# A MoE router with the tokens in the partitions, and a first expert that is selected straight from the counts

## What is computed

```python
def moe_ffn(h, w_router, w_gate, w_up, w_down):
    logits = (h @ w_router).astype(jnp.float32)
    top_logit, top_idx = lax.top_k(logits, TOP_E)
    gates = jax.nn.softmax(top_logit, axis=-1)
    combine = jnp.sum(jax.nn.one_hot(top_idx, N_EXP, dtype=jnp.float32) * gates[..., None], axis=-2)
    out = jnp.zeros_like(h)
    for e in range(N_EXP):
        out = out + combine[..., e:e + 1].astype(h.dtype) * swiglu(h, w_gate[e], w_up[e], w_down[e])
    return out
...
            h = h + moe_ffn(rms_norm(h, od_norm_ffn[i]), od_w_router[i], od_w_gate_e[i], od_w_up_e[i],
                            od_w_down_e[i])
```

## Time and profile before

| | us |
|---|---|
| three runs | 1521.80, 1523.29, 1526.05; median 1523.29 |
| the profiled execution | 1521.72, its span 1519.9 |
| PE busy in the span | 1431.6 (94%) |
| DVE, ACT, POOL busy | 1176.7, 1000.3, 74.6 |
| first transpose of x of block 1 | at 486.66 |
| first matmul of `gather_first` | at 505.09 |
| first matmul of `job(0)` | at 518.93 |

### The profile page before, as it was taken

The page is one execution under the profiler, slowest core; times in us unless marked ns, Lnnn a source line. Parts: engine busy times, 40 slices in busy tenths (PEclk is TensorE's granted clock), DMA queues, the critical chain, the costliest instruction groups (busy, mean ns, idle before and its releaser), DMA issues.

```text
span 1519.9 us, 18914 instructions
## 1 busy us (share of the span) xinstructions
PE 1431.6 (94%) x6676; PEld 1172.7 (77%) x6676; DVE 1176.7 (77%) x1139; ACT 1000.3 (66%) x975; POOL 74.6 (5%) x101
## 2 busy tenths in 40 slices
PE   7988999999888699999999999999999999999996
PEld 6766888887666578878878878887887887887885
DVE  5854555556554698889888888889888988888887
ACT  6554643435564577777777777787777777777776
POOL 1010100001341200000000000000000000000000
PEclk9999999999999699999999999999999999999998
DMA  9511865545332499999989989999999999998993
...
DMA packets 218360, 438.49 MB, mean 288 GB/s; under 512 B 7230, under 2 KB 11376, under 8 KB 218320
## 3 DMA queue, kind: packets, MB, share of 16 engines
...
...
## 4 chain that ended last, share of the span: by engine, by line
PE 86%; DVE 6%; issue 4%; ACT 3%; POOL 1%; DMA 0%; DVEq 0%; ACTq 0%; POOLq 0%
PE bank L1572 26%; PE bank L1567 26%; PE bank L1568 26%; DVE w_lo L952 2%; PE bank L2144 2%; ACT w_hi L436 1%; POOL pr L903 1%; PE bank L1742 1%; PE bank L2182 1%; PE bank L1801 1%; DVE w_lo L945 0%; PE bank L2098 0%; PE bank L2106 0%; PE bank L1808 0%; DVE key_mask L1127 0%
## 5 line engine op out<-in xcount | busy, mean ns | idle before, releaser
L952 DVE TENSOR_TENSOR w_lo<-raw,w_hi 128x2048 fp32r<-128x2048 f32 x339 | 768.7, 2288 | 84.4 <-ACT w_hi L443 83.2
L443 ACT ACTIVATE w_hi<-raw 128x2048 fp32r<-128x2048 f32 x339 | 649.5, 1919 | 185.5 <-PE bank L1572 185.5
L1567 PE MATMUL bank<-w_hi,xg_hi 128*128 128x512 f32 x896 | 355.4, 397 | 0.6 <-issue 0.6
L1568 PE MATMUL bank<-w_hi,xg_lo 128*128 128x512 f32 x896 | 350.2, 391 | 0.0
L1572 PE MATMUL bank<-w_lo,xg_hi 128*128 128x512 f32 x896 | 241.3, 391 | 10.1 <-DVE w_lo L952 10.1
L1567 PE MATMUL bank<-w_hi,ht_hi 128*128 128x512 f32 x528 | 207.4, 393 | 2.5 <-issue 2.5
L1568 PE MATMUL bank<-w_hi,ht_lo 128*128 128x512 f32 x528 | 206.5, 391 | 0.0
L1572 PEld LDWEIGHTS bank<-w_lo,xg_hi 128*128 128x128 f32 x896 | 168.0, 188 | 48.6 <-DVE w_lo L952 13.5
L1567 PEld LDWEIGHTS bank<-w_hi,xg_hi 128*128 128x128 f32 x896 | 168.8, 188 | 35.2 <-issue 0.7
L1568 PEld LDWEIGHTS bank<-w_hi,xg_lo 128*128 128x128 f32 x896 | 169.0, 189 | 33.7
L945 DVE TENSOR_TENSOR w_lo<-raw,w_hi 128x2048 fp32r<-128x2048 f32 (+4 forms) x65 | 144.4, 2232 | 43.9 <-ACT w_hi L436 43.8
...
## 6 DMA issues: line engine op xcount, KB each, us to landing
...
```

The lines of the kernel that those rows point to most:

```text
L443: act.activation(w_hi[:, g % HL, :], raw[:, g % RAW, :], ACT.Copy).then_inc(hi_ready, 1)
L952: dve.tensor_tensor(w_lo[:, g % HL, :], raw[:, g % RAW, :], w_hi[:, g % HL, :].bitcast(F32), ALU.subtract)\
L1567: pe.matmul(out_ap, l_hi, r_hi, start=first, stop=False)
L1568: pe.matmul(out_ap, l_lo, r_hi, start=False, stop=False)
```

## The change

The tokens become the stationary operand of the router, 128 of them at a time, and the 8 columns of `w_router` the moving one; so the logits come out with the tokens in the partitions, block by block, and no copy and no transpose are needed. `router(0)` stands before the transposes of block 1. DVE does `two_best(b)` for each block. The counting matmuls take float32r operands (`tri_r`, `ones_r`, `chose_r`), whose zeros and ones are exact, and one pass each. `sel` of the first expert is made from its own column of the counts; the rest of `spot`, then `place`, the gates and the over-full experts follow behind it on DVE. `xn` is now x times the gain row (from DVE, before the root is known), and the inverse root comes in as a scale where `xn_hi` and `xn_lo` are made; the gather is done for all of `xn_hi` first and for `xn_lo` after it into banks of its own, so that `xg_hi` and `xg_lo` are plain copies. ACT scales `xn` for the scatter, which POOL did before. The first three expert tiles are split earlier or elsewhere: `job_lo(0, 0)` before block 0 is filled, `job_lo(0, 1)` between the two `two_best`, `job_lo(0, 2)` behind the copies of `xg_lo`. The gain row is loaded without a wait for `x_added`.

```diff
+            act.activation(ident_r, ident, ACT.Copy).then_inc(wr_split, 1)
...
+            job_hi(0, 0)
             fill_block(0, lambda c: G_FFN1 + c)
+            job_hi(0, 1)
             fill_block(1, lambda c: G_FFN1 + c)
             act.wait_ge(x_added, 8)
             token_squares(6)
             root(6, 2)
+            act.wait_ge(inv_ready, 8)
             for b in range(T):
-                act.wait_ge(src_ready, b + 1)
-                act.activation(xn_hi[:, b], xn[:, b], ACT.Copy).then_inc(xn_split, 1)
-            act.activation(ident_r, ident, ACT.Copy).then_inc(wr_split, 1)
-            for i in range(AHEAD):
-                job_hi(0, i)
-            act.wait_ge(chosen, 1)
+                act.wait_ge(rows_gained, b + 1)
+                act.activation(xn_hi[:, b], xn[:, b], ACT.Copy, scale=stat[:, 6 + b:7 + b]).then_inc(xn_split, 1)
+            job_hi(0, 2)
+
+            for k in range(2):
+                act.wait_ge(hi_gathered, k + 1)
+                act.activation(xg_hi[:, 4 * k:4 * k + 4, :], B[1 + 2 * k].rearrange("p (c t) -> p c t", c=4), ACT.Copy)\
+                   .then_inc(xg_hi_ready, 1)
+            for b in range(T):
+                act.wait_ge(xn_split_lo, b + 1)
+                act.activation(xn[:, b], xn[:, b], ACT.Copy, scale=stat[:, 6 + b:7 + b]).then_inc(rows_scaled, 1)
+            act.wait_ge(chosen, 2)
...
-            pool.wait_ge(x_added, 5)
             pool.dma_start(gain_row, a["od_norm_ffn"].to_broadcast([P, D])).then_inc(gain_row_landed, 16)
 
 
-            pool.wait_ge(gain_row_landed, 16)
-            pool.wait_ge(xn_split_lo, 2)
-            for b in range(T):
-                pool.tensor_tensor(xn[:, b], xn[:, b], gain_row, ALU.mult).then_inc(rows_scaled, 1)
...
+            dve.tensor_scalar(iota_1, iota, 1.0, None, ALU.add).then_inc(iota_ready, 1)
+            dve.wait_ge(wr_split, 4)
             dve.tensor_tensor(wr_lo[:, :, :], wr[:, :, :], wr_hi[:, :, :].bitcast(F32), ALU.subtract).then_inc(wr_split_lo, 1)
             add_out(1, 0)
+            job_lo(0, 0)
+            dve.wait_ge(gain_row_landed, 16)
+
+            def gain_rows_of(b):
+
+                dve.wait_ge(x_added, 6 + 2 * b)
+                dve.tensor_tensor(xn[:, b], x[:, b], gain_row, ALU.mult).then_inc(rows_gained, 1)
+
+            gain_rows_of(0)
             fill_block(0, lambda c: G_FFN1 + c)
             add_out(1, 1)
+            gain_rows_of(1)
             fill_block(1, lambda c: G_FFN1 + c)
-            norm_tokens(6)
...
-            dve.wait_ge(logits_t, 1)
-            dve.tensor_copy(logit_rows, B[0][0:N_EXP, 0:S]).then_inc(logits_out, 1)
-            dve.wait_ge(logits, 1)
-            link(dve.tensor_copy(lg, B[6][:, 0:16].rearrange("p (b e) -> p b e", b=T)))
-            for b in range(T):
+            def two_best(b):
+
+                dve.wait_ge(logits, b + 1)
+                link(dve.tensor_copy(lg[:, b], B[b][:, 0:8]))
                 link(dve.max(top[:, b], lg[:, b]))
                 link(dve.max_index(top_i[:, b], top[:, b], lg[:, b]))
-            dve.tensor_copy(pick, top_i[:, :, 0:2])
+                link(dve.tensor_copy(pick[:, b], top_i[:, b, 0:2]))
+                dve.tensor_scalar(pick_0[:, b], iota_e, pick[:, b, 0:1], None, ALU.is_equal)
+                link(dve.tensor_scalar(tmp[:, b], iota_e, pick[:, b, 1:2], None, ALU.is_equal))
+                dve.tensor_tensor(chose_r[:, b], pick_0[:, b], tmp[:, b], ALU.add).then_inc(chosen, 1)
+
+            two_best(0)
+            inverse_root(6, 2, 2)
+            job_lo(0, 1)
+            two_best(1)
             link(dve.tensor_tensor(gap, top[:, :, 1], top[:, :, 0], ALU.subtract))
             link(dve.tensor_tensor(gap, gap, stat[:, 6:8], ALU.mult))
+            chose = chose_r[:, :, :].bitcast(F32)
+            dve.wait_ge(iota_ready, 1)
+            dve.wait_ge(places, 1)
             for b in range(T):
-                dve.tensor_scalar(pick_0[:, b], iota_e, pick[:, b, 0:1], None, ALU.is_equal)
-                link(dve.tensor_scalar(tmp[:, b], iota_e, pick[:, b, 1:2], None, ALU.is_equal))
-            dve.tensor_tensor(chose, pick_0, tmp, ALU.add).then_inc(chosen, 1)
+                link(dve.scalar_tensor_tensor(spot[:, b, 0:1], B[6 + b][:, 0:1], 1.0, chose[:, b, 0:1], ALU.add, ALU.mult))
+            for b in range(T):
+                one = dve.tensor_scalar(sel[:, b, :], iota_1, spot[:, b, 0:1], None, ALU.is_equal)
+            one.then_inc(sel_ready, 1)
             for b in range(T):
                 dve.wait_ge(xn_split, b + 1)
-                dve.tensor_tensor(xn_lo[:, b], xn[:, b], xn_hi[:, b].bitcast(F32), ALU.subtract).then_inc(xn_split_lo, 1)
-
-            dve.wait_ge(places, 1)
+                dve.scalar_tensor_tensor(xn_lo[:, b], xn[:, b], stat[:, 6 + b:7 + b], xn_hi[:, b].bitcast(F32),
+                                         ALU.mult, ALU.subtract).then_inc(xn_split_lo, 1)
+
+            dve.wait_ge(counted, 1)
+            link(dve.tensor_copy(cnt, B[5][:, 0:8]))
             for b in range(T):
-                link(dve.tensor_scalar(spot[:, b], B[7][:, 8 * b:8 * b + 8], 1.0, None, ALU.add))
-            link(dve.tensor_copy(cnt, B[7][:, 16:24]))
-            link(dve.tensor_tensor(spot, spot, chose, ALU.mult))
+                link(dve.scalar_tensor_tensor(spot[:, b], B[6 + b][:, 0:8], 1.0, chose[:, b], ALU.add, ALU.mult))
+            link(dve.tensor_scalar(ov, cnt, float(P), None, ALU.is_gt))
+            link(dve.tensor_tensor_scan(cum, ones[:, 0:8], ov, 0.0, ALU.mult, ALU.add))
+            link(dve.tensor_tensor(rank, cum, ov, ALU.mult))
+            link(dve.memset(number, 0.0))
+            dve.tensor_copy(number[:, 0:1], cum[:, 7:8])
+            for o in range(MAX_OVER):
+                one = dve.tensor_scalar(this[:, o], rank, float(o + 1), None, ALU.is_equal)
+            link(one)
+            link(dve.tensor_tensor(over_e, this, iota_e.unsqueeze(1).to_broadcast([P, MAX_OVER, 8]), ALU.mult))
+            link(dve.tensor_reduce(number[:, 1:1 + MAX_OVER], over_e, AX.X, ALU.add))
+            dve.tensor_copy(over[:, :], number[:, 0:5]).then_inc(routed, 1)
+            for k in range(2):
+                dve.wait_ge(gathered, k + 1)
+                one = dve.tensor_copy(xg_lo[:, 4 * k:4 * k + 4, :], B[2 * k].rearrange("p (c t) -> p c t", c=4))
+            one.then_inc(xg_lo_ready, 1)
+            job_lo(0, 2)
+
             link(dve.memset(place[:, :, :], -1.0))
             link(dve.memset(gate[:, :, :], 0.0))
             link(dve.tensor_scalar(place[:, :, 0:8], spot, -1.0, None, ALU.add))
-            select(0)
-            for i in range(AHEAD):
-                job_lo(0, i)
-
             dve.wait_ge(gate_exp, 1)
             link(dve.tensor_scalar(small(34, 2), gap, 1.0, None, ALU.add))
             link(dve.reciprocal(small(36, 2), small(34, 2)))
@@ -1456,25 +1478,13 @@
                 link(dve.scalar_tensor_tensor(mix[:, b], tmp[:, b], moe_s[:, 32 + b:33 + b], pick_0[:, b], ALU.mult, ALU.add))
                 link(dve.tensor_scalar(mix[:, b], mix[:, b], moe_s[:, 36 + b:37 + b], None, ALU.mult))
             dve.tensor_copy(gate[:, :, 0:8], mix)
-            take_first()
+            def router(b):
+
+                if b == 0:
+                    pe.wait_ge(wr_split_lo, 1)
+                for c in range(KC):
+                    pe.wait_ge(fill_lo, FILL_MOE + KC * b + c + 1)
+                    x_hi, x_lo = xt_hi[:, c, b * P:b * P + P], xt_lo[:, c, b * P:b * P + P]
+                    m = three(B[b][:, 0:N_EXP], x_hi, x_lo, wr_hi[:, c, :], wr_lo[:, c, :], c == 0, c == KC - 1)
+                m.then_inc(logits, 1)
+
+            router(0)
             pe.wait_ge(x_added, 8)
             fill_block(1)
-            pe.wait_ge(wr_split_lo, 1)
-            for c in range(KC):
-                pe.wait_ge(fill_lo, FILL_MOE + KC + c + 1)
-                m = three(B[0][0:N_EXP, 0:S], wr_hi[:, c, :], wr_lo[:, c, :], xt_hi[:, c, :], xt_lo[:, c, :], c == 0, c == KC - 1)
-            m.then_inc(logits_t, 1)
-            pe.wait_ge(logits_out, 1)
-            for b in range(T):
-                m = pe.transpose(B[6][:, 8 * b:8 * b + 8], logit_rows[:, b * P:b * P + P], ident[0:N_EXP, 0:N_EXP])
-            m.then_inc(logits, 1)
+            router(1)
+            pe.wait_ge(wr_split, 4)
             pe.wait_ge(chosen, 1)
-            pe.wait_ge(ones_set, 1)
-            m0, m1 = moe_s[:, 48:56], moe_s[:, 56:64]
-            pe.matmul(B[7][:, 0:8], tri, m0, start=True, stop=True)
-            pe.matmul(B[7][:, 8:16], tri, m1, start=True, stop=False)
-            pe.matmul(B[7][:, 8:16], ones[:, :], m0, start=False, stop=True)
-            pe.matmul(B[7][:, 16:24], ones[:, :], m0, start=True, stop=False)
-            pe.matmul(B[7][:, 16:24], ones[:, :], m1, start=False, stop=True).then_inc(places, 1)
-
-            def gather_first(half):
-
-                if half == 0:
-                    pe.wait_ge(sel_ready, 1)
```

(25 more changed lines are left out.)

65 lines of the change are left out of this document (21 added, 44 removed).

## The result

| | before | changed |
|---|---|---|
| median, us | 1523.43 (5 executions, 1521.8 to 1528.12) | 1513.70 (5 executions, 1511.25 to 1515.35) |
| profiled execution, us | 1521.72, span 1519.9 | 1515.35, span 1513.5 |
| ratio | 1 | 0.993, 95% interval 0.9909 to 0.995 |

The changed kernel is faster by 9.7 us by the medians, 6.4 us by the two profiled executions. The forecast was 12.0 off, and a median of 1511.3. The question is where the other 2.3 to 5.6 us are.

The account below looks back on a forecast made before the run. PE, busy 94%, bounds the kernel, so an earlier `job(0)` moves the end: 6.2 us before the gather plus 5.8 behind it make 12.0, 1523.3 to 1511.3; likeliest case 1508 to 1515, with parts of two rivals 1506.5 to 1516.

Parts of the forecast that it names:

- Before the router, and the 1.0 us of delay: Stretch up to block 1's transposes: router products at 0.11 us each start these at 487.7 instead of 486.66, 1.0 late.
- half the price: Lower bound on a router product: half of 0.11 us if the 128-column load can be hidden better.
- two passes: Router products at double price, as plain float32 counts; as a rival, gain 4.9 us, 1518.4, chance 0.08.
- From there to the gather: Block 1's transposes to the first gather product: gather at 498.9 in place of 505.1, 6.2 us earlier.
- the clock falling before the transposes (up to 1.3 less): Bound inside the forecast: half clock already before block 1's transposes, taking up to 1.3 us off the gain.
- From the gather to the job: First gather product to first product of `job(0)`: 8.05 us where 13.84 lay, 5.8 us more gained.
- Behind it: After the job's start: routing's rest ends 515.5, tile 3's `w_lo` 517.8, wanted at 519.2, so 1.4 us cover.
- No gain: Rival: time given back in `job(0)` because `w_lo` of tiles 3 and on come late; about 1523, chance 0.05.
- half clock in the gather and 4.4 us beyond the job's start: Assumed granted clock: 0.50 through the gather and the first 4.4 us of `job(0)`, until about 511.
- the clock comes back early: Rival: full clock from the gather on, job at 505.05, gain 16.1 us, 1507.2; chance 0.09.
- slower: Rival: clock stays at half in `job(0)`; for 42 tiles a net loss of 88 us, 1611; chance 0.03.
- the median's own scatter of 1.5: Bound inside the forecast: 1.5 us allowed for scatter of the measured median.

Follow-up runs that it names:

- pool_apart: Kernel before, with POOL's two gain-row products made to wait until the expert plan (`routed`) is written; median 1520.36 us against 1525.38, ratio 0.9967.
- xn_lo_first: Changed kernel with the two `xn_lo` subtractions put back ahead of `sel`, behind `two_best(1)`; one execution, 1512.0 us.
- counts_fp32: Changed kernel with the five counting products in plain float32 again, two passes each; one execution, 1513.57 us.
- lo1_ahead: Changed kernel with `job_lo(0, 1)` moved from between the two choices to behind the second gain-row product; median 1511.41 us, ratio 0.9923 to the kernel before.
- router0_behind: Changed kernel with the router of block 0 moved behind the transposes of block 1; median 1511.56 us against 1523.13 of the kernel before, ratio 0.993.
- after_again: Changed kernel run once more unaltered, for a second profile; median 1511.89 us against 1525.38 of the kernel before, ratio 0.9921.
- warm_a: Changed kernel with 20 unread 512-column products: 5 behind block 1's transposes, 12 behind `router(1)`, 3 behind the counts; median 1512.18 us, ratio 0.9916 to the kernel before.
- lo1_warm: Changed kernel with `job_lo(0, 1)` moved ahead of both choices and 17 unread 512-column products (5, 9, 3); median 1514.06 us, ratio 0.9929 to the kernel before.

## Why the prediction was right, and what was off

- *Before the router, and the 1.0 us of delay*: right. T is 0.98 later (3.50 for 2.52), a router product streams 8 columns and takes 0.11 at full clock and 0.21 at half, as a gather product does, which has the same load and streams 128; so the load of 128 columns rules it. Neither bound (half the price, two passes) is left. The gain row was loaded with cover; the products with it did not show on the path.
- *From there to the gather*, 6.2 forecast, 6.37 measured, of which 3.4 are the stretched instructions (pool_apart), 2.1 `xn_lo` behind `sel` (xn_lo_first), and 0.2 the one-pass counts (counts_fp32). The first was measured on the kernel before and the other two on the changed one, and that they add up is taken, not shown. The remaining 0.7 is the net of the turn of the logits and the making of `place`, gone, and the 2.3 of `job_lo(0, 1)` and the 1.0 of delay, added. lo1_ahead and router0_behind show how little of the two added terms could be saved alone: 0.4 of the first, since PE's router at half clock stands just behind it, and nothing of the second, since the second choice then waits for its logits. The bound "the clock falling before the transposes (up to 1.3 less)" came true in after_again and cost 0.4.
- *From the gather to the job*, 5.8 forecast, 5.88 measured. `over` was written 2.3 us ahead of the gather's end, as forecast (503.7 for 506.0). Of the two ends that the forecast found within its precision, the last copy to `xg_lo` (506.7) and the turn of `sel` with its 1.21 us (506.95), the copy is the later one: PE waits 0.44 for it behind the turn, and still 0.83 in warm_a.
- *Behind it*: the rest of the routing was mis-sized, "some 36 small instructions, 6.5 us" measured 5.3 (515.15 to 520.47), since many are not linked and start 0.1 apart. `w_lo` of tile 3 ended at 517.3 on the old axis (forecast 517.8), PE's one wait for `w_lo` at the start of the job is 1.27 us as before, and from 640 us on it is still 8.9 in 7. *No gain* is excluded: the time was not given back there.
- *The clock*: "half clock in the gather and 4.4 us beyond the job's start". The gather was at 0.50 (7.10 us, forecast 7.06), so *the clock comes back early* did not happen. The 4.4 was off by 1.6 in the first profile; the changed kernel and its edits without extra products show 2.8 to 5.9 us, with 1000.3 to 1001.7 us behind J. The moment scatters by more than the forecast's "1 us sooner or later", and is worth up to 1.4 us. The rival *slower* did not happen; the job's 512-column products brought the clock up in all three profiles. By the rule of the Trainium skill that the prediction weighed (TensorE: Matmul & The Clock Gate, What's actually happening) 7 us of gather without a gap would release the clock; it did not in any of these profiles, and neither did the 4.19 us of 512-column products of lo1_warm. In warm_a, where twelve 512-column products stood ahead of the gather, the clock was up.
- *The sum*: 12.0 forecast; the stretch gave 12.25, 11.86 and 12.25. Against this stands 9.7 in the first medians. The term of the sum that was mis-sized is "the median's own scatter of 1.5": an execution's clock falls in the attention stages move U by 5.6 us in the same program, so the median of so few can lie 2 us off: those of the kernel before in four comparisons run from 1523.13 to 1525.38. It had been read from three executions alone. It is larger than the errors of all other terms together (0.25 in J, 0.6 behind it, both to the good): 1513.70 was measured first, 1511.89 and 1511.48 in the next two comparisons, around the forecast 1511.3. That the stages ahead cost the changed kernel something lasting is not shown, and a difference under about 1 us there could not be seen. So what bears the forecast out is the stretch, whose parts were each met within 0.2 us, and not where the first median fell.

What stays open: why the clock falls at one softmax in one execution and not in the next. Between 400 and 440 us PE has the same two pauses, 4.4 us in all, in both profiles of the kernel before; the clock stayed at 1.00 in one and fell behind each pause in the other.
